# Gathering and bringing back in the experts: whole products against couples on halves of the array

## The chip, the cores and the metric

The kernel runs on one core of a Trainium2 chip, as one program of 34411 recorded instructions. The metric is the device time of one execution in microseconds (us), the median of several runs. TensorE (PE in the profile; PEld is its loading of weights) multiplies, ScalarE (ACT) and VectorE (DVE) prepare its operands and empty its results, SyncE (SP) starts the transfers from memory.

## The reference, cut to what matters

A block of two layers on 256 tokens of width 1024, and then a second block of two layers. The part at issue is the mixture of experts at the end of the first block:

```python
def moe_swiglu(h, router, w_gate, w_up, w_down):
    t = h.reshape(-1, d)                              # 256 tokens, d = 1024
    logits = (t @ router).astype(jnp.float32)         # 8 experts
    top_v, top_i = lax.top_k(logits, TOP_K)           # TOP_K = 2
    top_w = jax.nn.softmax(top_v, axis=-1)
    gates = jnp.sum(jax.nn.one_hot(top_i, N_EXPERTS, dtype=jnp.float32) * top_w[..., None], axis=1)
    out = jnp.zeros(t.shape, jnp.float32)
    for e in range(N_EXPERTS):
        y_e = swiglu(t, w_gate[e], w_up[e], w_down[e]).astype(jnp.float32)   # hidden width 3584
        out = out + gates[:, e:e + 1] * y_e
    return out.astype(h.dtype).reshape(bsz, seq, d)
```

## The kernel before, in words

The experts take the stretch from about 505 to 1491 us of the span. An expert works on at most 128 tokens, those that chose it. They are picked out by a product with a one-hot matrix (gathering) and its results are put back to their tokens by a product with the transposed one-hot matrix (bringing back). All large products are split: an operand is kept as a high part and a low part (type fp32r, which TensorE streams at one pass), and `split_product` (L203 to L205) adds three products, high with high, high with low, low with high.

**Steps.** The experts are run in pairs, `q` counts experts and `p` pairs; here the loop `with pe.Fori(0, pairs)` runs 3 times and a last pair stands behind it, 8 experts in all. An expert's hidden width is cut into NC = 7 chunks of 512 columns. A chunk is "gate" (24 products of 512 columns, in two halves of 12), the transposes of the chunk before (`turn`, L2943), "up" (24 products) and "down" of the chunk before (24 products). Each piece of weights comes in two halves of 1 MB; ScalarE rounds a half to its high part (`hi`, L3086, tile weights_hi, about 1.9 us), VectorE subtracts to get the low part (`lo`, L3184, weights_lo, about 2.3 us), and TensorE waits for that with `r_lo`. There are three places for such halves; `r_used` frees them.

**Gathering** (`gather(p, part)`, L2907 to L2921). Part 0 gathers the high parts of the tokens (xn_hi), part 1 the low parts (xn_lo), for both experts of pair `p` at once. The 1024 features are 8 tiles `k` of 128, the 256 tokens `NT` = 2 tiles `t` of 128, the contraction. For each of four banks there are two `k` and for each of them two products (t = 0, 1) of 256 columns, that is 4 products for a bank and 16 for a part. The banks are `HI_BANKS` 5, 6, 7, 1 and `LO_BANKS` 2, 5, 6, 7. After a bank's four products `r_gath` is counted up, and ScalarE copies the bank to x_pair (`gathered`, L3091), counting `r_xg`; banks 5, 6, 7 of part 1 wait for the copy of part 0 from the same bank. The first gather (pair 0) runs before the loop, both parts in one go, and VectorE copies the last two of its low banks (L3307) before TensorE may begin the first expert. The others run at the end of each odd expert of the loop, part 0 before and part 1 between the halves of its last "down".

**Bringing back** (`between` and `bring_back`, L2967 to L2985). After an expert the first "gate" of the next one is computed, then two banks (5, 6: tokens 0 to 127) of the results are brought back, then the first "up", then the other two banks (7, 2). Each bank takes two products of 512 columns, one with the high results `r.yh` (L2984) and one with the low ones `r.yl` (L2985), both with 128 rows of the one-hot matrix; in the profile these results carry the name x_parts. `r_scat` counts banks; VectorE adds them to the residual with the gate as a factor (`add`, L3221). There are 7 of these; the eighth expert has its own, `last_back` (L3046, L3047).

**The order** on each engine is the order in which the code is written; engines wait only by semaphores. A product's weights are loaded by an instruction of its own, ahead of it. A wait against a loop's number is computed by a register instruction in TensorE's sequencer, ahead of the product.

Elsewhere in the kernel, the attention of the first layer has heads of 64: the scores (`score`, L1655) multiply over 64 rows, heads alternately on the upper and the lower half, and wait for the copy at L1905. The weighted sums (L1700) fill 64 columns of the array at a time.

Of the kernel before, what the change touches and what calls it, by code (L numbers as in the profile page):

```python
# [23 lines left out]
P = 128  # L24
SEQ, D = 256, 1024
NT = SEQ // P
KT = D // P
HALF = 512
# [21 lines left out]
NC = FE // FC  # L50
# [2831 lines left out]
HI_BANKS, LO_BANKS = (5, 6, 7, 1), (2, 5, 6, 7)  # L2882
# [9 lines left out]
def moe_pe(pe, m):  # L2892
    s, r, c = m.sig, moe_mem(m), m.c
# [12 lines left out]
    def gather(p, part):  # L2906

        first = isinstance(p, int)
        if part == 0:
            pe.wait_ge(s["r_oh"], p + 1)  # L2910
        if first:
            pe.wait_ge(s[("r_xnh", "r_xnl")[part]], NT)
        for i, bank in enumerate((HI_BANKS, LO_BANKS)[part]):
            if part == 1 and i:
                pe.wait_ge(s["r_xg"], i if first else p * 8 + i - 2)
            for k in (2 * i, 2 * i + 1):
                for t in range(NT):
                    last = pe.matmul(m.ps[bank][:, (k % 2) * 2 * P:(k % 2 + 1) * 2 * P],  # L2918
                                     (r.xnh, r.xnl)[part][:, t, k * P:(k + 1) * P], r.oh[:, t, :],
                                     start=(t == 0), stop=(t == NT - 1))  # L2920
            last.then_inc(s["r_gath"], 1)  # L2921

    def halves(q, kind, ch, k, parts=(0, 1)):
        number, place, _, _ = moe_piece(kind, ch)
# [5 lines left out]
    def inner(q, side, bank, kind, ch):  # L2930
        mine = slice(side * P, (side + 1) * P)
        for half, (hi, lo) in halves(q, kind, ch, KT // 2):
            for j in range(KT // 2):
                k = half * KT // 2 + j
                last = split_product(pe, m.ps[bank][:, :], (r.xg[0][:, k, mine], r.xg[1][:, k, mine]),
                                     (hi[:, j, :], lo[:, j, :]), start=(k == 0), stop=(k == KT - 1))
            last.then_inc(s["r_used"], 1)
# [30 lines left out]
    def between(q, p, side):  # L2968

        if side == 1:  # L2970
            pe.wait_ge(s["r_xg"], p * 8 + 14)
        inner(q + 1, 1 - side, 0, "gate", 0)
        bring_back(q, p, side, 0)
        inner(q + 1, 1 - side, 1, "up", 0)
        bring_back(q, p, side, 1)

    def bring_back(q, p, side, t):
        if t == 0:
            pe.wait_ge(s["r_ohT"], p + 1)
            pe.wait_ge(s["r_yl"], 2 * q + 2)  # L2980
        for half in range(2):
            bank, cols = m.ps[((5, 6), (7, 2))[t][half]], slice(half * HALF, (half + 1) * HALF)
            rows = r.ohT[:, side, t * P:(t + 1) * P]
            pe.matmul(bank[:, :], rows, r.yh[:, cols], start=True, stop=False)  # L2984
            pe.matmul(bank[:, :], rows, r.yl[:, cols], start=False, stop=True).then_inc(s["r_scat"], 1)  # L2985

    def ending(q, side):

# [21 lines left out]
    def odd(q, p):  # L3010
        chunk(q, 1, 1, first=True)
        with pe.Fori(2, NC) as ch:
            chunk(q, 1, ch)
        pe.wait_ge(s["r_silu"], q * NC + NC)
        turn(q * NC + NC - 1)
        pe.wait_ge(s["r_ohT"], p + 1)
        gather(p + 1, 0)
        down(q, NC - 1, parts=(0,))
        gather(p + 1, 1)
        down(q, NC - 1, final=True, parts=(1,))  # L3020
# [28 lines left out]
    for part in range(2):  # L3049
        gather(0, part)  # L3050
# [6 lines left out]
    with pe.Fori(0, pairs) as p:  # L3057
        even(p * 2, p)
        between(p * 2, p, 0)
        odd(p * 2 + 1, p)  # L3060
        between(p * 2 + 1, p, 1)
    even(pairs * 2, pairs)
    between(pairs * 2, pairs, 0)
    odd_last(pairs * 2 + 1)
    pe.wait_ge(s["r_ohT"], pairs + 1)
# [8 lines left out]
def pair_of(bank):  # L3074
    return bank[:, :].rearrange("p (k s) -> p k s", k=2)

def moe_act(act, m):
    s, r = m.sig, moe_mem(m)
# [7 lines left out]

    def gathered(p, part, which=range(4)):
        for i in which:
            act.wait_ge(s["r_gath"], p * 8 + 4 * part + i + 1)  # L3090
            act.activation(r.xg[part][:, 2 * i:2 * i + 2, :], pair_of(m.ps[(HI_BANKS, LO_BANKS)[part][i]]),  # L3091
                           ACT.Copy).then_inc(s["r_xg"], 1)

# [45 lines left out]
    def odd(q, p):  # L3139
        with act.Fori(1, NC) as c:  # L3140
            chunk(q, c)
        hi(q, "down", NC - 1)
        hidden_hi(q * NC + NC - 1)
        hi(q + 1, "gate", 0, halves=(0,))
        gathered(p + 1, 0)
        gathered(p + 1, 1)
        hi(q + 1, "gate", 0, halves=(1,))
        y_hi(q)
        hi(q + 1, "up", 0)
        silu(q + 1, 0)  # L3150

    hi(0, "gate", 0, halves=(0,))
    experts_high(act, m, 1)
    hi(0, "gate", 0, halves=(1,))
    gathered(0, 0)
    gathered(0, 1, (0, 1))
    hi(0, "up", 0, halves=(0,))
# [19 lines left out]
def moe_dve(dve, m):  # L3177
    s, r, c = m.sig, moe_mem(m), m.c
    def lo(q, kind, ch, halves=(0, 1)):
        number, place, slot, _ = moe_piece(kind, ch)  # L3180
        for half in halves:
            dve.wait_ge(s["r_hi"], q * PIECES + number + half + 1)
            i = (place + half) % PLACES
            dve.tensor_tensor(m.wlo[i][:, :], r.slot[slot + half], m.whi[i][:, :],  # L3184
                              ALU.subtract).then_inc(s["r_lo"], 1)
# [8 lines left out]
    def hidden(q, ch):  # L3194
        dve.wait_ge(s["r_used"], moe_used(q, "up", ch))
        dve.wait_ge(s["r_silu"], q * NC + ch + 1)
        dve.tensor_tensor(r.h, r.silu, m.ps[1][:, :], ALU.mult).then_inc(s["r_h"], 1)

    def hidden_lo(i, hi=r.hh, out=r.hl):
        dve.wait_ge(s["r_hh"], i + 1)  # L3200
        dve.tensor_tensor(out, heads4(m.ps[2]), hi, ALU.subtract).then_inc(s["r_hl"], 1)

    def chunk(q, ch, last=False):
        hidden(q, ch - 1)
        lo(q, "up", ch)
        lo(q, "down", ch - 1, halves=(0,))
        hidden_lo(q * NC + ch - 1)
        lo(q, "down", ch - 1, halves=(1,))
        if not last:
            lo(q, "gate", ch + 1)  # L3210
# [5 lines left out]
            dve.tensor_tensor(r.yl[:, cols], m.ps[3 + side][:, :], r.yh[:, cols], ALU.subtract).then_inc(s["r_yl"], 1)  # L3216

    def add(q, t, half, last=False):
        dve.wait_ge(s["r_scat"], 4 * q + (2 * half + t if last else 2 * t + half) + 1)
        x = m.res[:, t, half * HALF:(half + 1) * HALF]  # L3220
        return dve.scalar_tensor_tensor(x, m.ps[((5, 6), (7, 2))[t][half]][:, :], r.gates[:, t, bass.ds(q, 1)], x,  # L3221
                                        ALU.mult, ALU.add)
# [17 lines left out]
        following(q)  # L3240

    def odd(q):
        with dve.Fori(1, NC - 1) as ch:
            chunk(q, ch)
        chunk(q, NC - 1, last=True)
        hidden(q, NC - 1)
# [56 lines left out]
    experts_low(dve, m, 1)  # L3303
    lo(0, "gate", 0, halves=(0,))
    for i in (2, 3):
        dve.wait_ge(s["r_gath"], 4 + i + 1)
        dve.tensor_copy(r.xg[1][:, 2 * i:2 * i + 2, :], pair_of(m.ps[LO_BANKS[i]])).then_inc(s["r_xg0"], 1)  # L3307
    lo(0, "gate", 0, halves=(1,))
    lo(0, "up", 0)
# [602 lines left out]
```

## Time and profile before

| | before |
|---|---|
| median of 3 runs | 2421.79 us |
| lowest and highest run | 2421.69 and 2421.97 us |
| span of the profiled execution, first to last instruction | 2419.4 us |
| what the runs have beyond that span | 2.4 us |
| TensorE busy | 2398.0 us, 99% |
| VectorE and ScalarE busy | 1893.5 us (78%) and 1440.4 us (60%) |
| granted clock of TensorE | 0.999 |

No total is recorded for the profiled execution beside its span; the runs stand for it. TensorE's products are pipelined: a product's duration in the profile reaches from its start to its modelled end and overlaps the next ones. What counts is the distance from start to start, called pitch below. In the timeline neighbouring instructions of the same kind stand in one row with their number; the pitch is the row's time less one duration, divided by the number less one.

### The profile page before, as it was taken

What the parts mean: (1) busy time and instruction counts of PE and PEld (TensorE: products, weight loads), DVE (VectorE), ACT (ScalarE), POOL (GpSimd) and SP (SyncE); (2) the same over time, 40 slices, a digit from 0 to 9 for tenths busy, and PEclk for the clock granted to TensorE, in tenths of its full rate; (3) what the DMA queues carried; (4) which work ended last, traced back from release to release, by engine and by line L of the source; (5) the groups of instructions that cost most, each with busy time, mean ns of one, the idle gap of its engine ahead of it and who ended that gap; (6) DMA issues with size and microseconds to landing.
All of it is one profiled execution on the core that took longest, in us unless ns stands there. A gap on an engine that the chain in (4) does not pass through costs nothing.

```text
span 2419.4 us, 34411 instructions
## 1 busy us (share of the span) xinstructions
PE 2398.0 (99%) x12612; PEld 2031.4 (84%) x12612; DVE 1893.5 (78%) x1989; ACT 1440.4 (60%) x1477; POOL 6.5 (0%) x30
## 2 busy tenths in 40 slices
PE   8999999999999999999999999999999999999998
PEld 7788899888888888888888888888888888887887
DVE  7667686678988898889888988676966676688766
ACT  6645444567777777777777777455254454543444
POOL 1000000000000000000000000000000000000000
PEclk9999999999999999999999999999999999999999
DMA  8375142469999999999999996853355566533653
GB/s 299 117 248 184 61 139 71 148 211 378 363 373 336 362 364 376 337 362 359 380 336 370 361 373 227 284 197 122 131 175 190 185 232 226 174 129 123 194 192 126
DMA packets 314239, 593.76 MB, mean 245 GB/s; under 512 B 8880, under 2 KB 134960, under 8 KB 313904
## 3 DMA queue, kind: packets, MB, share of 16 engines
q1 hardware_dynamic: 314160, 592.70, 69.5%
q8 instruction: 50, 0.82, 0.1%
q14 instruction: 29, 0.24, 0.0%
HBM read 591.62 MB, written 1.05 MB: 245 GB/s over the span
## 4 chain that ended last, share of the span: by engine, by line
PE 94%; DVE 3%; ACT 1%; DMA 1%; DVEq 1%; issue 0%; SPq 0%; ACTq 0%
PE bank L203 20%; PE bank L204 19%; PE bank L205 19%; PE bank L1216 16%; PE bank L1220 8%; PE bank L3454 1%; PE bank L2943 1%; PE bank L3381 1%; PE bank L2228 1%; PE bank L2238 1%; DMA mslot<-in_e_w_in 1%; PE bank L2918 1%; PE bank L1712 1%; PE bank L1056 0%; PE bank L2147 0%; PE bank L2247 0%
## 5 line engine op out<-in xcount | busy, mean ns | idle before, releaser
L3184 DVE TENSOR_TENSOR weights_lo<-mslot,weights_hi 128x2048 fp32r<-128x2048 f32 x336 | 768.2, 2291 | 110.8 <-ACT weights_hi L3086 110.5
L3086 ACT ACTIVATE weights_hi<-mslot 128x2048 fp32r<-128x2048 f32 x336 | 644.2, 1920 | 228.4 <-PE bank L205 228.4
L1368 DVE TENSOR_TENSOR weights_lo<-scratch,weights_hi 128x2048 fp32r<-128x2048 f32 x165 | 377.3, 2289 | 166.5 <-ACT weights_hi L1361 166.4
L1216 PE MATMUL bank<-x_parts,weights_hi 128*128 128x512 f32 x1760 | 441.2, 393 | 1.8 <-DVE x_parts L919 1.8
L1216 PEld LDWEIGHTS bank<-x_parts,weights_hi 128*128 128x128 f32 x1760 | 319.5, 189 | 63.7 <-DVE x_parts L919 2.4
L203 PE MATMUL bank<-weights_hi,x_pair 128*128 128x512 f32 x896 | 356.6, 398 | 0.2 <-issue 0.2
L204 PE MATMUL bank<-weights_lo,x_pair 128*128 128x512 f32 x896 | 351.7, 393 | 0.0
L205 PE MATMUL bank<-weights_hi,x_pair 128*128 128x512 f32 x896 | 349.4, 390 | 0.0
L1361 ACT ACTIVATE weights_hi<-scratch 128x2048 fp32r<-128x2048 f32 x165 | 315.2, 1913 | 50.2 <-PE bank L205 49.2
L203 PE MATMUL bank<-weights_hi,hidden_hi 128*128 128x512 f32 x808 | 315.9, 391 | 0.0
L204 PE MATMUL bank<-weights_lo,hidden_hi 128*128 128x512 f32 x808 | 315.2, 390 | 0.0
L205 PE MATMUL bank<-weights_hi,hidden_lo 128*128 128x512 f32 x808 | 314.6, 389 | 0.0
L1384 ACT ACTIVATE xT<-bank 128x256 f32<-128x256 f32 x220 | 83.5, 382 | 290.2 <-PE bank L1220 290.0
L1220 PEld LDWEIGHTS bank<-x_parts,weights_lo 128*128 128x128 f32 x1760 | 239.6, 190 | 17.1 <-DVE weights_lo L1368 0.4
L1220 PE MATMUL bank<-x_parts,weights_lo 128*128 128x256 f32 x1760 | 246.1, 283 | 0.0
L205 PEld LDWEIGHTS bank<-weights_hi,x_pair 128*128 128x128 f32 x896 | 168.2, 188 | 38.3
L203 PEld LDWEIGHTS bank<-weights_hi,x_pair 128*128 128x128 f32 x896 | 168.3, 188 | 36.6 <-issue 0.5
L204 PEld LDWEIGHTS bank<-weights_lo,x_pair 128*128 128x128 f32 x896 | 168.6, 188 | 32.8
L205 PEld LDWEIGHTS bank<-weights_hi,hidden_lo 128*128 128x128 f32 x808 | 151.7, 188 | 32.1
L203 PEld LDWEIGHTS bank<-weights_hi,hidden_hi 128*128 128x128 f32 x808 | 151.9, 188 | 30.6
L204 PEld LDWEIGHTS bank<-weights_lo,hidden_hi 128*128 128x128 f32 x808 | 151.9, 188 | 29.6
L1457 DVE TENSOR_TENSOR xT<-bank,xT 128x256 f32<-128x256 f32 x110 | 45.4, 420 | 57.4 <-ACT xT L1384 57.4
(550 smaller groups left out, 2789.5 us busy)
## 6 DMA issues: line engine op xcount, KB each, us to landing
mslot<-in_o_moe_w_gate SPq DMA_DIRECT2D x112, 1024.0 KB, 5.5
mslot<-in_o_moe_w_up SPq DMA_DIRECT2D x112, 1024.0 KB, 5.6
mslot<-in_o_moe_w_down SPq DMA_DIRECT2D x112, 1024.0 KB, 5.7
scratch<-in_ffn_w_gate SPq DMA_DIRECT2D x44, 1024.0 KB, 5.4
scratch<-in_ffn_w_up SPq DMA_DIRECT2D x44, 1024.0 KB, 5.4
scratch<-in_ffn_w_down SPq DMA_DIRECT2D x44, 1024.0 KB, 5.1
mslot<-in_o_w_in SPq DMA_DIRECT2D x7, 2048.0 KB, 8.7
scratch<-in_e_ffn_w_gate SPq DMA_DIRECT2D x11, 1024.0 KB, 5.4
```

The source lines that it names most:

```text
L203: pe.matmul(out, stationary[0], moving[0], start=start, stop=False)
L204: pe.matmul(out, stationary[0], moving[1], start=False, stop=False)
L205: return pe.matmul(out, stationary[1], moving[0], start=False, stop=stop)
L1216: pe.matmul(m.ps[bank + j][:, :], hi[:, k, cols(j)], both, start=(k == 0), stop=False)
L1220: last = pe.matmul(m.ps[bank + j][:, 0:SEQ], lo[:, k, cols(j)], m.xh[:, k, :], start=False, stop=(k == KT - 1))
L1361: act.activation(m.whi[ffn_place(v, kind, u)][:, :], m.fslot[i], ACT.Copy).then_inc(m.sig["f_hi"], 1)
L1368: dve.tensor_tensor(m.wlo[to][:, :], m.fslot[i], m.whi[to][:, :], ALU.subtract).then_inc(m.sig["f_lo"], 1)
L1384: act.activation(out[:, cols], m.ps[bank + j][:, SEQ:2 * SEQ], ACT.Copy).then_inc(s[copied], 1)
L1457: dve.tensor_tensor(f.ulow[:, cols], m.ps[2 + j][:, 0:SEQ], f.ulow[:, cols], ALU.add)
L1712: last = pe.matmul(m.ps[EVEN_OUT[2 * t + half]][:, :], e.yT[:, k, t * P:(t + 1) * P], mblock(m, B_EVEN + 4 + half)[:, k, :], start=(start ...
L3086: act.activation(m.whi[(place + half) % PLACES][:, :], r.slot[slot + half], ACT.Copy).then_inc(s["r_hi"], 1)
L3184: dve.tensor_tensor(m.wlo[i][:, :], r.slot[slot + half], m.whi[i][:, :], ALU.subtract).then_inc(s["r_lo"], 1)
```

## The change

Each product of the gathering and of the bringing back (of `last_back` not) is written as two over 64 rows of the contraction: partitions 0 to 63 on the upper rows of the array, 64 to 127 on the lower. Two banks are worked on at a time: the upper half of one with the lower half of the other, couple after couple. For each of the two pairs of banks this is done first one way, `(0, 1), (2, 3)`, and then the other, `(1, 0), (3, 2)`, so that each bank gets both halves. A new semaphore `r_tile` says that a half has finished its bank's first turn, and the second turn waits for it. `r_gath` and `r_scat` are counted in the second turns only, and those that wait for them wait for two banks together. The bringing back is one block after "gate". VectorE's loop over an odd expert's chunks has its first pass written out.

```diff
@@ gather @@
-        for i, bank in enumerate((HI_BANKS, LO_BANKS)[part]):
-            if part == 1 and i:
-                pe.wait_ge(s["r_xg"], i if first else p * 8 + i - 2)
-            for k in (2 * i, 2 * i + 1):
+        banks, rows = (HI_BANKS, LO_BANKS)[part], (r.xnh, r.xnl)[part]
+        left = set(range(4))
+        for upper, lower in ((0, 1), (2, 3), (1, 0), (3, 2)):
+            if upper > lower:
+                pe.wait_ge(s["r_tile"], (0 if first else p * 16 - 4) + 4 * part + upper + 1)
+            if part == 1 and upper + lower in (1, 5) and upper < lower:
+                freed = max(upper, lower)
+                pe.wait_ge(s["r_xg"], freed if first else p * 8 + freed - 2)
+            for j in range(2):
                 for t in range(NT):
-                    last = pe.matmul(m.ps[bank][:, (k % 2) * 2 * P:(k % 2 + 1) * 2 * P],
-                                     (r.xnh, r.xnl)[part][:, t, k * P:(k + 1) * P], r.oh[:, t, :],
-                                     start=(t == 0), stop=(t == NT - 1))
-            last.then_inc(s["r_gath"], 1)
+                    for i, tile in sorted(((upper, slice(0, P // 2)), (lower, slice(P // 2, P)))):
+                        begins = i in left
+                        left.discard(i)
+                        k = 2 * i + j
+                        last = pe.matmul(m.ps[banks[i]][:, j * 2 * P:(j + 1) * 2 * P], rows[tile, t, k * P:(k + 1) * P],
+                                         r.oh[tile, t, :], start=begins, stop=False, skip_group_check=True)
+                        if j == 1 and t == NT - 1:
+                            last.then_inc(s["r_gath" if upper > lower else "r_tile"], 1)
@@ between @@
         inner(q + 1, 1 - side, 0, "gate", 0)
-        bring_back(q, p, side, 0)
+        bring_back(q, p, side)
         inner(q + 1, 1 - side, 1, "up", 0)
-        bring_back(q, p, side, 1)
@@ bring_back @@
-        if t == 0:
-            pe.wait_ge(s["r_ohT"], p + 1)
-            pe.wait_ge(s["r_yl"], 2 * q + 2)
-        for half in range(2):
-            bank, cols = m.ps[((5, 6), (7, 2))[t][half]], slice(half * HALF, (half + 1) * HALF)
-            rows = r.ohT[:, side, t * P:(t + 1) * P]
-            pe.matmul(bank[:, :], rows, r.yh[:, cols], start=True, stop=False)
-            pe.matmul(bank[:, :], rows, r.yl[:, cols], start=False, stop=True).then_inc(s["r_scat"], 1)
+        pe.wait_ge(s["r_ohT"], p + 1)
+        pe.wait_ge(s["r_yl"], 2 * q + 2)
+        left = set(range(4))
+        for upper, lower in ((0, 1), (2, 3), (1, 0), (3, 2)):
+            if upper > lower:
+                pe.wait_ge(s["r_tile"], p * 16 + 8 + 12 * side + upper + 1)
+            for y in (r.yh, r.yl):
+                for i, tile in sorted(((upper, slice(0, P // 2)), (lower, slice(P // 2, P)))):
+                    t, half = i // 2, i % 2
+                    begins = i in left
+                    left.discard(i)
+                    last = pe.matmul(m.ps[(5, 6, 7, 2)[i]][:, :], r.ohT[tile, side, t * P:(t + 1) * P],
+                                     y[tile, half * HALF:(half + 1) * HALF], start=begins, stop=False,
+                                     skip_group_check=True)
+                    if y is r.yl:
+                        last.then_inc(s["r_scat" if upper > lower else "r_tile"], 1)
@@ gathered (ScalarE) @@
-            act.wait_ge(s["r_gath"], p * 8 + 4 * part + i + 1)
+            act.wait_ge(s["r_gath"], p * 8 + 4 * part + i // 2 * 2 + 2)
@@ add (VectorE) @@
-        dve.wait_ge(s["r_scat"], 4 * q + (2 * half + t if last else 2 * t + half) + 1)
+        dve.wait_ge(s["r_scat"], 4 * q + (2 * half + t + 1 if last else 2 * t + 2))
@@ odd (VectorE) @@
-        with dve.Fori(1, NC - 1) as ch:
+        chunk(q, 1)
+        with dve.Fori(2, NC - 1) as ch:
@@ the first gather's low banks (VectorE) @@
-        dve.wait_ge(s["r_gath"], 4 + i + 1)
+        dve.wait_ge(s["r_gath"], 4 + i // 2 * 2 + 2)
```

TensorE at part 0 of a gather in the loop, before (the transposes of `turn`, the gather, the next "down"; the number behind x counts products):

```order
L2943 MATMUL bank2<-consts,xT 128x128 x3
L2910 REGISTER_ALU [waits r_ohT]
L2918 MATMUL bank5<-one_hot,xn_hi 128x256 [waits r_oh]
L2918 MATMUL bank5<-one_hot,xn_hi 128x256 x3
L2918 MATMUL bank6<-one_hot,xn_hi 128x256 x4
L2918 MATMUL bank7<-one_hot,xn_hi 128x256 x4
L2918 MATMUL bank1<-one_hot,xn_hi 128x256 x4
L2926 REGISTER_ALU [waits r_hl]
L203 MATMUL bank3<-weights_hi1,hidden_hi 128x512 [waits r_lo]
```

The same place in the change, the end of the second pair of banks and the first of the turned ones (each row is one half over 64 rows):

```order
L2927 MATMUL bank1<-one_hot,xn_hi 128x256
L2927 MATMUL bank7<-one_hot,xn_hi 128x256
L2927 MATMUL bank1<-one_hot,xn_hi 128x256
L2917 ISA
L2927 MATMUL bank5<-one_hot,xn_hi 128x256 [waits r_tile]
L2927 MATMUL bank6<-one_hot,xn_hi 128x256
L2927 MATMUL bank5<-one_hot,xn_hi 128x256
L2927 MATMUL bank6<-one_hot,xn_hi 128x256
L2927 MATMUL bank5<-one_hot,xn_hi 128x256
L2927 MATMUL bank6<-one_hot,xn_hi 128x256
L2927 MATMUL bank5<-one_hot,xn_hi 128x256
L2927 MATMUL bank6<-one_hot,xn_hi 128x256
```

Where a bank had its four products in a row, two banks now alternate, and a bank's second turn stands eight halves behind its first and waits for `r_tile`.

TensorE where results are brought back after an odd expert, before (end of "gate", the first two banks, begin of "up"):

```order
L205 MATMUL bank0<-weights_hi1,x_pair 128x512
L2980 ISA [waits r_ohT]
L2984 MATMUL bank5<-x_parts,one_hot_T 128x512 [waits r_yl]
L2985 MATMUL bank5<-x_parts,one_hot_T 128x512
L2984 MATMUL bank6<-x_parts,one_hot_T 128x512
L2985 MATMUL bank6<-x_parts,one_hot_T 128x512
L2926 REGISTER_ALU
L203 MATMUL bank1<-weights_hi2,x_pair 128x512 [waits r_lo]
```

In the change:

```order
L205 MATMUL bank0<-weights_hi1,x_pair 128x512
L2988 ISA [waits r_ohT]
L2998 MATMUL bank5<-x_parts,one_hot_T 128x512 [waits r_yl]
L2998 MATMUL bank6<-x_parts,one_hot_T 128x512
L2998 MATMUL bank5<-x_parts,one_hot_T 128x512
L2998 MATMUL bank6<-x_parts,one_hot_T 128x512
L2998 MATMUL bank7<-x_parts,one_hot_T 128x512
L2998 MATMUL bank2<-x_parts,one_hot_T 128x512
L2998 MATMUL bank7<-x_parts,one_hot_T 128x512
L2998 MATMUL bank2<-x_parts,one_hot_T 128x512
L2992 REGISTER_ALU
L2998 MATMUL bank5<-x_parts,one_hot_T 128x512 [waits r_tile]
```

All four banks now stand between "gate" and "up", and the block behind "up" is gone.

## Rows read from the trace of the kernel before

**Rows 1.** The page's line of busy time, and the core's span and clock.
```profile
PE 2398.0 (99%) x12612; PEld 2031.4 (84%) x12612; DVE 1893.5 (78%) x1989; ACT 1440.4 (60%) x1477; POOL 6.5 (0%) x30
core 0: 2419.4 us, clock 0.999
```

**Rows 2.** Groups of products (line, names, shapes, count | busy, mean ns | idle before).
```profile
L203 PE MATMUL bank<-weights_hi,x_pair 128*128 128x512 f32 x896 | 356.6, 398 | 0.2 <-issue 0.2
...
L2984 PE MATMUL bank<-x_parts,one_hot_T 128*128 128x512 f32 x28 | 10.9, 389 | 0.0
...
L2918 PE MATMUL bank<-one_hot,xn_lo 128*128 128x256 f32 x64 | 8.3, 283 | 0.0
```

**Rows 3.** Timeline of TensorE, first gather in the loop (start us, us, ...).
```profile
746.98 0.60 PE L2943 MATMUL bank<-consts,xT 128*128 128x128 f32 x4
747.33 2.15 PE L2918 MATMUL bank<-one_hot,xn_hi 128*128 128x256 f32 x16
749.43 0.49 PE L203 MATMUL bank<-weights_hi,hidden_hi 128*128 128x512 f32 x1
749.76 0.39 PE L204 MATMUL bank<-weights_lo,hidden_hi 128*128 128x512 f32 x1
...
752.05 0.39 PE L205 MATMUL bank<-weights_hi,hidden_lo 128*128 128x512 f32 x1
752.28 2.08 PE L2918 MATMUL bank<-one_hot,xn_lo 128*128 128x256 f32 x16
754.19 0.40 PE L203 MATMUL bank<-weights_hi,hidden_hi 128*128 128x512 f32 x1
```

**Rows 4.** Timeline of TensorE, half a bringing back.
```profile
638.28 0.39 PE L2984 MATMUL bank<-x_parts,one_hot_T 128*128 128x512 f32 x1
...
639.19 0.39 PE L203 MATMUL bank<-weights_hi,x_pair 128*128 128x512 f32 x1
```

**Rows 5.** Timeline of TensorE, from whole products to 64 rows.
```profile
42.67 0.28 PE L205 MATMUL bank<-scratch_parts 128*128 128x256 f32 x1
42.88 2.89 PE L1655 MATMUL bank<-scratch 64*128 64x128 f32 x32
```

**Rows 6.** Timeline of TensorE: couples of 128 and 256 columns; whole products of 256.
```profile
42.88 1.16 PE L1655 MATMUL bank<-scratch 64*128 64x128 f32 x16
43.88 1.90 PE L1655 MATMUL bank<-scratch 64*128 64x256 f32 x16
...
61.09 1.89 PE L1622 MATMUL bank<-xT,mslot 128*128 128x256 f32 x8
```

**Rows 7.** Timeline of TensorE and of its loads, from 64 columns to whole products.
```profile
69.41 0.55 PE L1700 MATMUL bank<-xT,scratch 128*64 128x128 f32 x6
...
69.89 0.30 PEld L1712 LDWEIGHTS bank<-mslot,scratch 128*128 128x128 f32 x2 [0.17 <-issue]
70.43 0.19 PEld L1712 LDWEIGHTS bank<-mslot,scratch 128*128 128x128 f32 x1 [0.24 <-issue]
```

**Rows 8.** Timeline of VectorE, the copy that the scores wait for.
```profile
41.55 0.69 DVE L1905 COPY scratch<-bank 128x512 f32<-128x512 f32 x1 [0.75 <-PE bank L1649]
```

**Rows 9.** Timelines of TensorE, ScalarE and VectorE, the gather before the loop.
```profile
508.43 2.17 PE L2918 MATMUL bank<-one_hot,xn_hi 128*128 128x256 f32 x16
509.65 3.02 ACT L3091 ACTIVATE x_pair<-bank 128x512 fp32r<-128x512 f32 x6
512.26 1.28 DVE L3307 CAST x_pair<-bank 128x512 fp32r<-128x512 f32 x2
513.64 0.47 PE L203 MATMUL bank<-weights_hi,x_pair 128*128 128x512 f32 x1 [0.25 <-issue]
```

**Rows 10.** Timelines of ScalarE, VectorE and TensorE behind the first gather in the loop.
```profile
752.95 2.07 ACT L3091 ACTIVATE x_pair<-bank 128x512 fp32r<-128x512 f32 x4 [0.99 <-PE bank L2918]
754.88 1.93 ACT L3086 ACTIVATE weights_hi<-mslot 128x2048 fp32r<-128x2048 f32 x1
756.85 2.29 DVE L3184 TENSOR_TENSOR weights_lo<-mslot,weights_hi 128x2048 fp32r<-128x2048 f32 x1 [4.51 <-ACT weights_hi L3086]
759.68 0.39 PE L203 MATMUL bank<-weights_hi,x_pair 128*128 128x512 f32 x1
```

More of the change, by code:

```diff
@@ L2972, in between, with bring_back @@
         inner(q + 1, 1 - side, 0, "gate", 0)
-        bring_back(q, p, side, 0)
+        bring_back(q, p, side)
         inner(q + 1, 1 - side, 1, "up", 0)
-        bring_back(q, p, side, 1)
-    def bring_back(q, p, side, t):
-        if t == 0:
-            pe.wait_ge(s["r_ohT"], p + 1)
-            pe.wait_ge(s["r_yl"], 2 * q + 2)
-        for half in range(2):
-            bank, cols = m.ps[((5, 6), (7, 2))[t][half]], slice(half * HALF, (half + 1) * HALF)
-            rows = r.ohT[:, side, t * P:(t + 1) * P]
-            pe.matmul(bank[:, :], rows, r.yh[:, cols], start=True, stop=False)
-            pe.matmul(bank[:, :], rows, r.yl[:, cols], start=False, stop=True).then_inc(s["r_scat"], 1)
+    def bring_back(q, p, side):
+        pe.wait_ge(s["r_ohT"], p + 1)
[14 more added lines that the diff above has]
+                        last.then_inc(s["r_scat" if upper > lower else "r_tile"], 1)
     def ending(q, side):
```

## The prediction

> **What bounds the kernel now.** I read the page first, then the timeline of TensorE around the two places that change, then ScalarE and VectorE in the same stretches. The page and the core's line give TensorE busy for 99% of a span of 2419.4 us at a granted clock of 0.999, so at 2.4 GHz throughout [rows 1]. Busy is not proof, but products follow one another without holes: the 896 of the first group wait 0.2 us in all [rows 2]. So what TensorE's stream gains or loses in the experts is, almost one to one, what the kernel gains or loses. The other engines matter only where they hold TensorE up.
>
> [Rows 3] show the first of the three gathers inside the loop: transposes, the sixteen high products, half a down step, the sixteen low products, the other half. Sixteen low products take 2.08 us, the last one 0.28 of it, so the pitch is (2.08 - 0.28) / 15 = **0.12 us**. A bringing back is four products, from 638.28 to 639.19: **0.23 us** each [rows 4]. Their neighbours keep the same pitches, so before the change both places sit in the stream with no seam. There are 128 gathering products and 56 of the bringing back that the change rewrites [rows 2].
>
> **What the change does to a product.** Every product over 128 rows becomes two over 64 rows, on two banks: 128 products become 128 couples, 56 become 56 couples. The adds per output are the same. A couple can only pay if its halves run together, and gain only if a couple is faster than one whole product. The kernel has such couples already: the attention scores, 64 rows each, alternately the upper and the lower half [rows 6]. Sixteen of them with 256 columns take 1.90 us, the last 0.38: eight couples at a pitch of (1.90 - 0.38) / 7 = 0.217. Whole products of 256 columns of the same type: (1.89 - 0.38) / 7 = 0.216. So a couple costs what a whole product costs, and both weight loads hide. These stream at half the rate of the split ones (0.216 against 0.12 for 256 columns), so type is the one difference. I take 0 for the exchange. Both ends: eight couples of 128 columns have a pitch of (1.16 - 0.27 - 0.21) / 6 = 0.11 [rows 6], which no gathering couple should beat, so -0.01; and +0.01 is the most that the rows' rounding and the second half's later start leave. Over 184 couples: -1.9 to +1.9 us.
>
> The Trainium skill ("TensorE: Matmul & The Clock Gate", Measured speedup vs the span model) has a pack last one product plus about 4 ns for each further tile. As an estimate from that figure, 184 couples would cost 0.7 us more than whole products, where the rows give nothing to the nearest 0.01 us; it stays inside the bounds and out of the sum.
>
> **What it costs to change between whole products and halves.** [Rows 5]: the last whole product starts at 42.67, the first load of the scores at 42.88, 0.21 later; in a stream the load starts with the product before. The 32 products last 2.89, of which 0.38 is the last; less 7 pitches of 0.11 and 8 of 0.217 that leaves 0.21 + 0.01 for the first gap, a load that nothing hides. So the second couple stands 0.42 after the last whole product, where a stream would have it 0.12 + 0.11 later: **0.19 us lost at the entrance**. At another change of shape, from 64 columns back to whole, the last product starts at 69.69 (69.41 + 0.55 - 0.27), the load at 69.89, and the second whole product starts with the load behind it at 70.43 [rows 7]: 0.74 for what would be 0.11 + 0.43 (two products at the pitches of these streams), **0.20 lost at the exit**. 
>
> For this kernel's places: a product of 512 split columns streams as long as 256 at half the rate, 0.21, so the load comes 0.31 after its start, the second couple 0.52, against 0.23 + 0.12: 0.17. Leaving, 0.20 to the load and 0.33 to the second product (749.43 to 749.76 shows 0.33 for an unhidden load) against 0.12 + 0.23: 0.18 after gathering; the same after a bringing back (0.64 against 0.46).
>
> **The sum.**
> 1. High gathers in the loop, 3 times. The last transpose starts at 747.31. Now: load 0.20 later, second couple at 747.72, sixteenth at 749.40, load of the down step 749.60, second product 749.93. Before: 749.76 [rows 3]. The seam that was there already (0.33 at 749.43, a wait for hidden_lo) is taken up in it. 3 x 0.17 = **0.5 us**.
> 2. Low gathers, 3 times, entrance 0.17 and exit 0.18: **1.1 us**.
> 3. Bringing back, 7 times. The two groups of four products are now one block after "gate" (shown by the second piece of order), so one entrance and one exit: 7 x 0.35 = **2.5 us**. The adds' results come sooner, the new copy of VectorE's first loop pass does no new work; VectorE has time there: 0.
> 4. The first gather. ScalarE could copy bank by bank from 509.65 on [rows 9]. Now r_gath counts only from the third group: the twelfth couple starts at 508.43 + 0.22 + 10 x 0.12 = 509.85, plus 0.28 and 0.03: first copy 510.16. A copy takes 0.5 ((3.02 - 0.6) / 5), so the third ends at 511.7. The low part's second group waits for that: its couples start at 511.75, 511.96, the last of the part at 513.16, done 513.47. VectorE's copies start then and not at 512.26, 1.2 later, and TensorE's 513.64 waits for their end [rows 9]: **1.2 us**.
> 5. The same lateness in the loop, 3 times. High copies: ScalarE is busy until 749.9 anyway, hidden. Low ones: the twelfth couple starts at 752.05 + 0.52 + 10 x 0.12 = 753.77, the copy at 754.08 and not 752.95, so 1.15 later. ScalarE's next part of the weights (754.88) and VectorE's weights_lo after it (756.85, ends 759.14) move by as much, to 760.29 [rows 10]. TensorE needs that for the product at 759.68. The one after it was at 759.91; the low gather's own 0.35 (item 2) puts it at 760.26. With the wait it starts at 760.29 + 0.05 + 0.33 = 760.67. 3 x 0.4 = **1.2 us**.
> 6. The two waits for r_tile in each block. In a gather four couples (0.48) lie between a half's end and its use, and it is done 0.28 after its start. In a bringing back there are two (0.46), and a product of 512 columns is done after 0.39, which leaves 0.07 and the 0.1 by which the load could be late unseen. 0, hidden by the second group. If that cover goes, each costs a load in the open, 0.10: at most 30 x 0.1 = 3.0.
>
> 0.5 + 1.1 + 2.5 + 1.2 + 1.2 = **6.5 us** over a span of 2419.4. The runs lie at 2421.7 to 2422.0, 2.4 above this span, for what lies around it. So 2421.8 + 6.5 = **2428.3 us**, +0.27%. The whole interval is 6.5 - 4.1 - 1.9 and less (no emptying, below) to 6.5 + 1.9 + 3.0 = 11.4.
>
> **Rivals.**
> *No emptying: not slower.* The 0.2 us in [rows 5, 7] could belong to their waits on a semaphore, even one met long ago, or to their type. Then items 1 to 3 vanish (4.1) and 4 and 5 stay: +2.4, 2424.2 us, and 2422.3 if couples are 0.01 faster each as well: no change that can be measured. It decides if the first load of a bringing back comes under 0.25 after the last gate product. Against it: two places show the same 0.20. The Trainium skill ("TensorEngine Tiling (Array Packing)", Key Properties) says that switching the mode drains TensorE; by that rule this rival falls, and it gives no price. Chance 0.18.
> *The swap waits bite.* r_tile is read by the sequencer after a REGISTER_ALU; if it comes late in the bringing back (margin 0.07), 14 times 0.1 to 0.2 come on top, 2429.7 to 2431.1; with all thirty waits 2431.3. Chance 0.11.
> *Halves don't overlap* with split types: 128 x 0.12 + 56 x 0.23 = 28 us more, 2456 us. [Rows 6] speak against it. Chance 0.04.
> *Faster.* With split types the halves could stream at twice the rate, as their half height might suggest: 28 / 2 = 14 us less, 2414 us. To beat items 1 to 5 by 4.8 us a couple would have to save 0.06; in [rows 6] it saves nothing, and the load's 0.11 stands under it. Chance 0.03, for what I overlook (an entrance hidden elsewhere, the moved DVE pass).
> My forecast has the rest, 0.64.
>
> **How the numbers follow.** 0.2% is 4.8 us, about what a measurement of this kernel can tell from no change. Of my 0.64 about 0.57 lies above it, with swap waits and no overlap 0.72. Same: the rival without emptying and my low end, 0.25. Faster: 0.03. The range takes in the no-emptying case at +2.2 and the top of the bounds: 2424.0 to 2433.2.
>
> **What would show it.** In the changed trace: L2927 and L2998 as 64-row products in couples, pitch 0.12 and 0.23; the first load of each block 0.3 after the product before (0.2 after transposes), the first load behind it 0.2; ScalarE's x_pair copies in the loop at about 754.2 instead of 752.95 (less the drift); a wait of TensorE for weights_lo of about 0.4 in the half after each low gather; 512.26 moved by 1.2. I am wrong if the loads at the seams come at once, if the pitch of a couple differs by over 0.01, or if TensorE waits at the third group of a bringing back.

## The result, and the profile after

| | before | after |
|---|---|---|
| median of 7 runs | 2421.79 us | 2429.23 us |
| lowest and highest run | 2421.63 and 2422.40 us | 2428.86 and 2429.69 us |
| span of the profiled execution | 2419.4 us | 2426.9 us |

The change makes the kernel **7.4 us slower**, a ratio of 1.0031 with a 95% interval of 1.0020 to 1.0042. The forecast was 2428.3 us, +6.5, in a range of 2424.0 to 2433.2. The profiled executions differ by 7.5 us, so the traces hold the whole difference.

The page's line of busy time and the core's line, against [rows 1]:

```profile
PE 2404.2 (99%) x12796; PEld 2030.5 (84%) x12796; DVE 1892.4 (78%) x1989; ACT 1440.1 (59%) x1477; POOL 6.6 (0%) x30
core 0: 2426.9 us, clock 1.000
```

The clock is the same. TensorE's busy time grew by 6.2 us with no more to compute: a product whose load nothing hides is recorded as busy for 0.50 us and not 0.39, so most of a seam counts as busy. The busy share, 99% in both, tells nothing of the loss.

The groups of products (columns as in [rows 2]):

```profile
L203 PE MATMUL bank<-weights_hi,x_pair 128*128 128x512 f32 x896 | 357.7, 399 | 0.9 <-DVE weights_lo L3201 0.5 <-issue 0.4
L2998 PE MATMUL bank<-x_parts,one_hot_T 64*128 64x512 f32 x112 | 14.8, 403 | 0.0
L2927 PE MATMUL bank<-one_hot,xn_lo 64*128 64x256 f32 x128 | 8.9, 286 | 0.5 <-ACT x_pair L3108 0.3
```

In the last two rows a product covers 64 rows by 128 columns. There are twice as many of these as before, and each is recorded about as long as a whole one (403 ns against 389, 286 against 283). A half saves nothing by being half.

TensorE at the first gather in the loop, which answers to [rows 3]:

```profile
748.72 0.60 PE L2952 MATMUL bank<-consts,xT 128*128 128x128 f32 x4
749.25 2.17 PE L2927 MATMUL bank<-one_hot,xn_hi 64*128 64x256 f32 x32
751.35 0.50 PE L203 MATMUL bank<-weights_hi,hidden_hi 128*128 128x512 f32 x1
751.69 0.40 PE L204 MATMUL bank<-weights_lo,hidden_hi 128*128 128x512 f32 x1
...
753.97 0.39 PE L205 MATMUL bank<-weights_hi,hidden_lo 128*128 128x512 f32 x1
754.29 2.17 PE L2927 MATMUL bank<-one_hot,xn_lo 64*128 64x256 f32 x32
756.39 0.50 PE L203 MATMUL bank<-weights_hi,hidden_hi 128*128 128x512 f32 x1
756.73 0.40 PE L204 MATMUL bank<-weights_lo,hidden_hi 128*128 128x512 f32 x1
```

Thirty-two halves take 2.17 us, less one duration 1.89 for 15 steps, of which the first is 0.22: the pitch of a couple is 1.67 / 14 = 0.12, that of a whole product before. What is new stands at both ends. The last transpose starts at 749.04 (748.72 + 0.60 - 0.27) and the first couple at 749.25, 0.20 later. The last high couple starts at 751.14 and the down step at 751.35, its second product 0.34 after that. Entering after a product of 512 columns takes longer, 753.97 to 754.29 = 0.32; that product streams for 0.23, the transpose for 0.11. Before, the same steps (transpose to gather, gather to down, down to gather) were 0.03, 0.23 and 0.23. The step out of the high part is not longer than before, because a load stood in the open there before the change too (0.33 to the second product, 749.43 to 749.76 in [rows 3]); what the high gather loses is all at its entrance.

The first bringing back, which answers to [rows 4]:

```profile
639.33 0.39 PE L205 MATMUL bank<-weights_hi,x_pair 128*128 128x512 f32 x1
639.65 2.11 PE L2998 MATMUL bank<-x_parts,one_hot_T 64*128 64x512 f32 x16
641.69 0.50 PE L203 MATMUL bank<-weights_hi,x_pair 128*128 128x512 f32 x1
642.03 0.40 PE L204 MATMUL bank<-weights_lo,x_pair 128*128 128x512 f32 x1
```

From the last gate product to the first couple 0.32 where there was 0.23, and from the last couple (639.65 + 2.11 - 0.39 = 641.37) to the second product of "up" 0.66 where there was 0.46.

### The profile page after: what moved, and what is told of

It reads as the page before. It is cut to its first block, busy times and chain, and to the rows that moved or that the text cites. A ratio compares the mean times of both kernels' runs of the same rounds, so it can differ in the third digit from the quotient of the medians.

```text
span 2426.9 us, 34761 instructions
## 1 busy us (share of the span) xinstructions
PE 2404.2 (99%) x12796; PEld 2030.5 (84%) x12796; DVE 1892.4 (78%) x1989; ACT 1440.1 (59%) x1477; POOL 6.6 (0%) x30
## 4 chain that ended last, share of the span: by engine, by line
PE 93%; DVE 3%; ACT 2%; DMA 1%; DVEq 1%; issue 0%; ACTq 0%; SPq 0%
PE bank L203 19%; PE bank L204 19%; PE bank L205 19%; PE bank L1216 16%; PE bank L1220 8%; PE bank L3472 1%; PE bank L2952 1%; PE bank L3399 1%; PE bank L2228 1%; PE bank L2238 1%; DMA mslot<-in_e_w_in 1%; PE bank L2927 1%; PE bank L2998 1%; PE bank L1712 1%; PE bank L1056 0%
```

## The experiments

Each kernel is compared with the kernel before on the same chip. For the stretches I use the traces: the time from the first gathering product to the transposes (L2943, L2952 or as the line may be) at four places. This leaves out what differs between executions ahead of the experts, about 0.3 us either way. The first column holds the first gather, the second adds a bringing back after an even expert, the third a gather in the loop and the bringing back behind it, the fourth all (four gathers and seven bringings back).

| later than before, us | behind the first gather | ahead of the first gather in the loop | behind it | end of the experts | median of the runs, and over before |
|---|---|---|---|---|---|
| the change | 1.33 | 1.78 | 3.25 | 7.72 | 2429.23, +7.4 |
| gathering alone in halves | 1.34 | 1.35 | 2.38 | 4.40 | 2425.89, +4.2 |
| bringing back alone in halves | 0.01 | 0.48 | 0.91 | 3.35 | 2424.91, +3.3 |
| whole products, late banks | 1.30 | 1.33 | 1.97 | 3.15 | 2425.00, +3.4 |
| whole products, one block | -0.02 | 0.05 | 0.05 | 0.30 | 2422.78, +1.0 |
| two blocks of halves | 1.33 | 2.24 | 4.10 | 10.76 | 2432.26, +10.6 |
| turns next to each other | 1.75 | 2.24 | 4.69 | 11.13 | 2432.45, +10.7 |
| neighbours on the same rows | 1.33 | 3.05 | 5.77 | 16.52 | 2438.33, +16.5 |

The kernel before had a median of 2421.65 in the runs beside the two parts alone, the late banks and the two blocks, and 2421.80 beside the other three.

### One half of the change at a time

```diff
 gathering alone: the change, and in bring_back, between and add the lines of before
-                pe.wait_ge(s["r_tile"], (0 if first else p * 16 - 4) + 4 * part + upper + 1)
+                pe.wait_ge(s["r_tile"], (0 if first else p * 8) + 4 * part + upper + 1)
 bringing back alone: the change, and in gather and those that wait for it the lines of before
-                pe.wait_ge(s["r_tile"], p * 16 + 8 + 12 * side + upper + 1)
+                pe.wait_ge(s["r_tile"], p * 8 + 4 * side + upper + 1)
```

> Only the gathering is in couples, the bringing back is as before (whole products, two blocks). Theory of seams and late banks: high gathers 3 x 0.19, low gathers 3 x 0.37, the wait for weights_lo behind each low gather 3 x 0.42, the first gather 1.3, so 4.3 us over before, about 2426.1. Rival, that the couples themselves cost (7.4 us spread over 184 couples, 0.04 each): 128 x 0.04 = 5.2, about 2427.0, with no wait behind the gather in particular.

> Only the bringing back is in couples, in one block; the gathering is as before. Theory of seams: 7 blocks x 0.43 (entrance 0.20, exit 0.20, couples 0.03) = 3.0 us over before, about 2424.8. Rival, that the couples themselves cost 0.04 each: 56 x 0.04 = 2.2, about 2424.0. The two parts should add to the whole: this and the gathering alone together 7.3 over before.

Measured: 2425.89 and 2424.91. The parts add up in the traces, 4.40 + 3.35 = 7.75 against 7.72. The rival that each couple itself costs 0.04 fails in the table. The 32 couples before the loop do make 1.34, but the 96 in the loop, 3.8 by that price, cost 4.40 - 1.34 = 3.06, of which a part is a wait on VectorE (next run), and the 56 couples of the bringing back, 2.2 by that price, cost 3.35. The cost goes by blocks, not by couples, as the next runs show.

### Late banks without halves

```diff
+        for turn_of, pair in ((0, (0, 1)), (0, (2, 3)), (1, (0, 1)), (1, (2, 3))):
+            for i in pair:
+                for j in range(2):
+                    k = 2 * i + j
+                    last = pe.matmul(..., rows[:, turn_of, k * P:(k + 1) * P], r.oh[:, turn_of, :], ...)
+                if turn_of == 1:
+                    last.then_inc(s["r_gath"], 1)
```

ScalarE and VectorE wait for two banks together here, as in the change.

> No halves at all. The gathering's whole products stand in the order of the turns (first 128 tokens of all four banks, then the other 128), so each bank is finished as late as in the change and is waited for in the same pairs. Theory: no seams; the first gather 1.2 us later; in the loop the copies start 0.96 later and TensorE, which is not late itself, waits 0.57 for weights_lo, 3 times: 2.9 us over before, about 2424.7. Rival, that the late copies cost nothing of their own and the seams are all: no change, 2421.8.

Measured: 2425.00, and 3.15 in the trace. So late banks cost 3.15 us with no halves at all: a bank is handed on when twelve or sixteen products are done and no longer after four. (In the change they cost somewhat less, as shown below.) TensorE's entrance and exit are without a seam here, and still it stands idle before the second half of "gate" (timelines of VectorE and TensorE):

```profile
758.93 2.29 DVE L3190 TENSOR_TENSOR weights_lo<-mslot,weights_hi 128x2048 fp32r<-128x2048 f32 x1 [5.47 <-ACT weights_hi L3092]
760.59 0.39 PE L205 MATMUL bank<-weights_hi,x_pair 128*128 128x512 f32 x1
761.28 0.51 PE L203 MATMUL bank<-weights_hi,x_pair 128*128 128x512 f32 x1 [0.30 <-DVE weights_lo L3190]
761.63 0.40 PE L204 MATMUL bank<-weights_lo,x_pair 128*128 128x512 f32 x1
```

VectorE's weights_lo ends at 761.22, and the product that needs it starts at 761.28, 0.69 after its neighbour in place of 0.23. In the change the same wait looks like this (ScalarE, VectorE, TensorE; before: [rows 10]):

```profile
756.05 2.07 ACT L3108 ACTIVATE x_pair<-bank 128x512 fp32r<-128x512 f32 x4 [2.35 <-PE bank L2927]
757.98 1.94 ACT L3103 ACTIVATE weights_hi<-mslot 128x2048 fp32r<-128x2048 f32 x1
759.95 2.29 DVE L3201 TENSOR_TENSOR weights_lo<-mslot,weights_hi 128x2048 fp32r<-128x2048 f32 x1 [5.88 <-ACT weights_hi L3103]
761.76 0.39 PE L205 MATMUL bank<-weights_hi,x_pair 128*128 128x512 f32 x1
762.30 0.51 PE L203 MATMUL bank<-weights_hi,x_pair 128*128 128x512 f32 x1 [0.15 <-DVE weights_lo L3201]
762.64 0.40 PE L204 MATMUL bank<-weights_lo,x_pair 128*128 128x512 f32 x1
```

ScalarE's copies come at 756.05, 3.1 after the 752.95 of before, where the whole kernel is 1.74 late there: 1.36 of their own. The part of the weights behind them comes as late, weights_lo too, and TensorE waits: 0.54 + 0.34 for what took 0.46, so **0.42**. Without halves the wait is longer, (0.69 + 0.35) - 0.46 = 0.58, since TensorE has no seams to be late by. The two costs partly pay for each other, which is why the gathering alone (4.40) is less than its seams (3 x 0.19 + 3 x 0.38) and this run's 3.15 together. In the change, late banks are 1.33 for the first gather and 3 x 0.42 in the loop, 2.6 us or a third of the loss.

Before the loop, TensorE, ScalarE and VectorE in the change (before: [rows 9]):

```profile
508.39 2.17 PE L2927 MATMUL bank<-one_hot,xn_hi 64*128 64x256 f32 x32
510.89 0.74 PE L2927 MATMUL bank<-one_hot,xn_lo 64*128 64x256 f32 x8 [0.34 <-ACT x_pair L3108]
511.78 1.70 PE L2927 MATMUL bank<-one_hot,xn_lo 64*128 64x256 f32 x24
510.15 2.07 ACT L3108 ACTIVATE x_pair<-bank 128x512 fp32r<-128x512 f32 x4 [0.45 <-PE bank L2927]
513.54 1.29 DVE L3325 CAST x_pair<-bank 128x512 fp32r<-128x512 f32 x2 [1.24 <-PE bank L2927]
514.93 0.47 PE L203 MATMUL bank<-weights_hi,x_pair 128*128 128x512 f32 x1 [0.44 <-issue]
```

The first copy comes at 510.15 and not 509.65. The low part is held until 510.89 and again until 511.78. VectorE's two copies start at 513.54 and not 512.26, and the first expert's first product 1.29 later than before; counted from the first gathering product, which here stands 0.04 earlier, that is the table's 1.33.

### More seams with the same products

```diff
@@ bring_back of the change @@
         for upper, lower in ((0, 1), (2, 3), (1, 0), (3, 2)):
+            if (upper, lower) == (1, 0):
+                inner(q + 1, 1 - side, 1, "up", 0, ahead=True)   # the first three products of up
```

> The change, with three products of the following up (its first split product) moved between the first and the second turns of each bringing back, so that there are two entrances and two exits and the same products. Theory of seams: 7 more pairs of seams at 0.40 = 2.8 us over the change, about 2432.0; the loads at the new seams come 0.31 after the product before. Rival, that a block costs for another reason (its first wait, a semaphore): 2429.2, and the new seams show loads at once.

Measured: 2432.26, 3.0 over the change; in the traces 10.76 - 7.72 = 3.04, which is 7 x 0.43. TensorE in the first bringing back:

```profile
639.36 0.39 PE L205 MATMUL bank<-weights_hi,x_pair 128*128 128x512 f32 x1
639.68 1.20 PE L3001 MATMUL bank<-x_parts,one_hot_T 64*128 64x512 f32 x8
640.81 0.50 PE L203 MATMUL bank<-weights_hi,x_pair 128*128 128x512 f32 x1
641.14 0.39 PE L204 MATMUL bank<-weights_lo,x_pair 128*128 128x512 f32 x1
641.37 0.40 PE L205 MATMUL bank<-weights_hi,x_pair 128*128 128x512 f32 x1
641.70 1.20 PE L3001 MATMUL bank<-x_parts,one_hot_T 64*128 64x512 f32 x8
642.83 0.51 PE L203 MATMUL bank<-weights_hi,x_pair 128*128 128x512 f32 x1
```

Both ways in start 0.32 or 0.33 after the product before, and both ways out have 0.33 or 0.34 to the second product. The semaphores asked for at the new seams were met long before: r_tile at the way in, and at the way out r_lo for weights that the three products between had already used. That a semaphore's wait, even a met one, makes the seam is ruled out by the next run. The seam belongs to the change of shape. Seven more pairs of seams cost seven times one pair.

### Where the block stands

```diff
         inner(q + 1, 1 - side, 0, "gate", 0)
         bring_back(q, p, side, 0)
+        bring_back(q, p, side, 1)
         inner(q + 1, 1 - side, 1, "up", 0)
-        bring_back(q, p, side, 1)
@@ odd (VectorE) @@
+        chunk(q, 1)
-        with dve.Fori(1, NC - 1) as ch:
+        with dve.Fori(2, NC - 1) as ch:
```

> The kernel before, with its two groups of four bringing-back products put in one block between gate and up, and VectorE's first pass of the odd expert's loop written out as in the change. Whole products. Theory: neither costs anything, 2421.8 within 0.3. Rival: the block's place or the written-out pass is part of the 7.4 us, 0.5 us or more over before.

Measured: 2422.78, but its ten runs spread from 2421.70 to 2423.32 and those of before beside it from 2420.87 to 2423.12; the interval of the ratio, 0.9993 to 1.0013, holds no change. The median is 1.0 higher, while the median span from first to last instruction is not (2419.55 against 2419.70): what differs lies outside that span. The trace gives 0.30 over the experts, 0.04 for each of the seven blocks. TensorE in the first bringing back:

```profile
638.39 0.39 PE L205 MATMUL bank<-weights_hi,x_pair 128*128 128x512 f32 x1
638.62 0.39 PE L2984 MATMUL bank<-x_parts,one_hot_T 128*128 128x512 f32 x1
...
640.21 0.39 PE L2985 MATMUL bank<-x_parts,one_hot_T 128*128 128x512 f32 x1
640.43 0.39 PE L203 MATMUL bank<-weights_hi,x_pair 128*128 128x512 f32 x1
```

The block stands in the same place as in the change, with the same waits for r_ohT and r_yl ahead of it and for r_lo behind it, and its steps in and out are 0.23 and 0.22: whole products have no seam there. The 0.04 is no seam either. It arises about 11 us later, at the product behind the next transposes, which waits for weights_lo. It comes from the block's place and not from VectorE's written-out pass: the run with the gathering alone has that pass and the old places, and nothing is added there behind a bringing back (1.34, then 1.35).

### The wait for r_tile without cover

```diff
@@ gather of the change @@
-        for upper, lower in ((0, 1), (2, 3), (1, 0), (3, 2)):
+        for upper, lower in ((0, 1), (1, 0), (2, 3), (3, 2)):
```

> The change, with the turns of the gathering in the order (0,1), (1,0), (2,3), (3,2): the second turn of a pair of banks follows its first at once, so the first two banks are done after 8 couples and not 12, and the wait for r_tile has no other couples to hide behind. Theory: each of the 16 waits in the open costs about 0.28 (end of a half) + 0.05 + 0.11 (load) - 0.12 = 0.3, so 16 x 0.3 = 4.9, less what earlier copies give back (the first gather's part of about 0.5; in the loop the low part starts its copies 0.2 earlier, 3 x 0.2): 3 to 4.5 us over the change, 2432 to 2434. Rival: r_tile is not felt even so (TensorE works in order), and the earlier copies gain 1 to 2 us against the change, 2427.5.

Measured: 2432.45, 3.2 over the change. The high part of the first gather in the loop takes 2.88 us where the change takes 2.17 (timeline of TensorE), and its loads stop twice (timeline of its loads):

```profile
749.53 2.88 PE L2927 MATMUL bank<-one_hot,xn_hi 64*128 64x256 f32 x32
```
```profile
749.53 0.53 PEld L2927 LDWEIGHTS bank<-one_hot,xn_hi 64*128 64x128 f32 x8 [0.17 <-issue]
750.36 1.01 PEld L2927 LDWEIGHTS bank<-one_hot,xn_hi 64*128 64x128 f32 x16 [0.29 <-PE bank L2927]
751.66 0.54 PEld L2927 LDWEIGHTS bank<-one_hot,xn_hi 64*128 64x128 f32 x8 [0.30 <-PE bank L2927]
```

The view of waits between 500 and 1500 us (in total, times, longest):

```profile
PEld bank L2927 <- PE bank L2927: 4.7, 16, 0.3
```

Sixteen waits of 0.3, 4.7 us, in which the loads stand idle: TensorE does wait for itself. In its stream of products a wait costs more, (2.88 - 2.17) / 2 = 0.35, since the load behind the wait is in the open as well; sixteen of them make 5.7. In the change the row of waits isn't there: the second pair of banks hides the wait, as item 6 of the prediction had it. The table has only 11.13 - 7.72 = 3.4 more than the change, so 2.3 come back. In the loop the three waits of 0.42 for weights_lo are gone, because TensorE itself is late enough. The first gather costs only 0.42 more (1.75 against 1.33) where four waits of 0.35 stand in it, so banks that are done earlier give back 1.0 there.

### Do halves run together?

```diff
@@ bring_back of the change @@
-        for upper, lower in ((0, 1), (2, 3), (1, 0), (3, 2)):
+        for second, pair in ((0, (0, 1)), (0, (2, 3)), (1, (0, 1)), (1, (2, 3))):
...
-                for i, tile in sorted(((upper, slice(0, P // 2)), (lower, slice(P // 2, P)))):
+                for i, tile in ((i, slice(second * P // 2, (second + 1) * P // 2)) for i in pair):
```

> The change, with the 16 halves of each bringing back in another order: the eight on the upper rows, then the eight on the lower, so that neighbours share rows and can't overlap. Theory (halves on different rows run together and each takes the time of a whole product): 8 more product times of 0.23 in each of 7 blocks, less one overlap: 7 x 7.5 x 0.23 = 12.1 us over the change, about 2441.3. Rival, that the array takes halves one after the other anyway or that a half alone is cheaper: less than 6 over the change.

Measured: 2438.33, 9.1 over the change and not 12.1. The theory's sign and the rival's failure are clear, its size isn't: 1.26 for each block, not 1.73. TensorE in the first bringing back:

```profile
639.58 0.39 PE L205 MATMUL bank<-weights_hi,x_pair 128*128 128x512 f32 x1
639.90 3.37 PE L2998 MATMUL bank<-x_parts,one_hot_T 64*128 64x512 f32 x16
643.20 0.50 PE L203 MATMUL bank<-weights_hi,x_pair 128*128 128x512 f32 x1
```

Sixteen halves, one after the other at 0.23, would start over 0.33 + 14 x 0.23 = 3.55 us. They start over 3.37 - 0.38 = 2.99: about two and a half products are saved. This happens in the middle of the block. Products of L2998 between 640.9 and 641.6 (count, shortest, median and longest in ns, first and last start):

```profile
L2998 PE MATMUL bank<-x_parts,one_hot_T x6: 383/394/496, 640.7 to 641.5; 64*128 64x512 f32 x6
```

Six products start between 640.7 and 641.5, where a pitch of 0.23 allows four. One of them is 0.496 long, the length of a product whose load nothing hides, as the first of the block has. It is the first on the lower rows. It waits for r_tile, which is counted by the third and the fourth upper product; the fourth starts at 640.70 and is over at 641.09. That the lower one starts at 641.15 and not when the eight upper ones are through (the trace has three of those starting at 641.16, 641.39 and 641.63) says that the two halves of the array go on by themselves, each in its own order. The expectation had reckoned with one queue, so 1.73 was too much. All seven blocks have a second product of that length 1.25 to 1.27 after their first.

## Why the prediction was right, point by point

The time was forecast at +6.5 and came at +7.4; all five terms were there, each at the place named, and all were a little small. The time alone would not have proved it: the range, from 2424.0 up, also held the rival without emptying (2424.2). The seams in the trace decide.

| item | forecast | measured | from |
|---|---|---|---|
| 1. high gathers, 3 | 3 x 0.17 | 3 x 0.19 | 748.72 to 751.69 against 746.98 to 749.76 |
| 2. low gathers, 3 | 3 x 0.35 | 3 x 0.38 | 753.97 to 756.73 against 752.05 to 754.42 |
| 3. bringing back, 7 | 7 x 0.35 | 7 x 0.43 | 639.33 to 642.03 = 2.70 against ten pitches of 0.2275 [rows 4]; 0.45 with the block's place in the table |
| 4. first gather | 1.2 | 1.33 | table |
| 5. wait for weights_lo, 3 | 3 x 0.4 | 3 x 0.42 | 761.76 to 762.64 |
| 6. r_tile | 0 | 0 | no such row |

(1: 2.97 against 2.78. 2: 2.76 against 2.37, which is 0.38 before rounding, and 754.42 is the product after 754.19.) The measured terms make 7.3 us, the trace has 7.7. Of the rest, 0.3 is the cost of the block's place, which the run with whole products in one block shows. Item 3 had put it at 0 ("VectorE has time there: 0"); it is small, but it isn't nothing. The last 0.1 was not followed.

*The step that was mis-sized* is the price of an entrance in front of couples of 512 columns. The prediction put the second couple 0.31 + 0.21 after the last whole product and used that for the bringing back as well. The 0.21 was read from couples of 128 columns [rows 5], where the step behind an open load is short; in front of couples of 512 columns it is 0.33, the value that the prediction itself used for the exit. An entrance is then 0.32 + 0.33 against 0.455, **0.20**, and an exit 0.32 + 0.34 against 0.455, 0.20. With 0.02 to 0.03 more for slightly slower couples (from the second to the eighth 1.38 us, where six whole products take 1.365) that makes 0.43, where 0.35 stood. Over seven blocks this is 0.6 of the 0.9 us that were missing.

*Two slips in the working* changed no term. The first gap in [rows 5] comes out as 0.22 with 7 pitches of 0.217, since sixteen couples have fifteen steps; with the 8 that stand there nothing would be left. And the copy in item 5 moves from 752.95 to 754.08, by 1.13 and not 1.15.

*The exchange itself* was forecast at 0 and is 0 in the gathering (0.12 against 0.12), 0.02 to 0.03 for a block in the bringing back. The fp32 couples of the attention were a fair stand-in for split ones. The Trainium skill ("TensorE: Matmul & The Clock Gate", Measured speedup vs the span model) names about 4 ns for a further tile, from which the estimate of 0.7 us was worked out; the trace has the second half of a couple 3 ns behind the first in the gathering, and the pitch did not grow by it.

*The emptying rival* would have shown the first load under 0.25 after the last gate product. It comes at 0.32 or 0.33, at all seven, and the run with two blocks repeats it at seams whose semaphores were met long before. Whole products in the same place, behind the same waits, have no seam. The rule of the Trainium skill ("TensorEngine Tiling (Array Packing)", Key Properties), that switching the mode drains TensorE, agrees with this trace, and the runs give its price: 0.20 us each way in a dense stream.

*The swap waits* were rightly left at 0 with cover. Without it they cost 0.35 each in the gathering and not the 0.1 that the prediction gave as its bound. That bound was too low: it counted only an open load and left out the time until the half that is waited for has ended.

## What to carry to other kernels

Couples on halves of the array do no more per time than whole products when the contraction is 128 long (measured here at 256 and 512 columns), so there is nothing for them to earn there. Each change of shape between blocks leaves TensorE without work for a moment, 0.2 us in and 0.2 us out here, so a short block of halves in a dense stream of whole products loses. And an order that finishes all banks together hands them on late: look at what copies those banks and what stands behind the copy in the same engine's order, since that was a third of the loss (2.6 us; 3.15 by itself) and had nothing to do with the array.

## What the runs showed of the hardware that I had not expected

The upper and the lower half of the array keep their own order: with all eight upper halves ahead of the lower ones in the program, the first lower one started before the last three upper ones, and about two and a half product times of 0.23 were saved in each block. A semaphore counted by the last product of a block should therefore not be taken to speak for the other half's products; the change counts both. That TensorE waits for its own semaphore, sixteen times in one run and at 0.35 us of its stream each time, belongs to the same point. What held the lower half back in that block was r_tile and not the upper products that the program has ahead of it, and such a wait isn't free. Whether two halves on one bank would keep their order without it, no run shows.
